# One packed array for constants, norm gains, router weights and biases, and narrower pooling matrices, in a two-layer encoder kernel

## What is computed

```python
for i in range(DEPTH):                                   # DEPTH = 2
    h = rms_norm(x, norm_mix_g[i])
    x = x + (pool_mixer(h, ...) if i == 0 else diff_attention(h, ...))
    h = rms_norm(x, norm_ffn_g[i])
    x = x + hier_moe(h, moe_wg[i], moe_bg[i], moe_we[i], moe_be[i], moe_w1[i], moe_w3[i], moe_w2[i])
return rms_norm(x, final_g)

def pool_mixer(h, w, scale):      # windows 2, 4, 8, 16; 256 channels each
    mix = (cs - lagged) / cnt[None, :, None] - hg        # windowed causal mean minus the token
    outs.append(einsum('bsc,cd->bsd', mix, w[gi]))       # then times scale

def hier_moe(...):
    g_prob = softmax(xf @ wg + bg); e_logits = xf @ we + be   # 4 groups, 8 experts in each
    ...                                                  # top group, top 2 experts in it, gates
    a = silu(xb @ w1[e]) * (xb @ w3[e]); y = a @ w2[e]   # for each expert
```

## Time and profile before

| | |
|---|---|
| runs | 1101.11, 1104.31 and 1104.18 us, median 1104.18 |
| profiled execution, from its first to its last instruction (span) | 1099.3 us |
| median less span | 4.9 us (between 1.8 and 5.0 for the three runs) |
| TensorE busy, mean granted clock | 79%, 0.932 of full speed |
| weight loads of TensorE busy | 47% |
| VectorE, ScalarE, GpSimd busy | 32%, 21%, 0.1% |
| DMA | 426.55 MB, 388 GB/s over the span |

### The profile page before, as it was taken

One profiled execution on the slowest core, in us unless ns is written; L12 is line 12 of the kernel. 1 busy time (PEld: TensorE's weight loads), 2 busy tenths in 40 slices (PEclk: granted clock), 3 DMA queues, 4 the chain that ended last, 5 costly groups with the idle time before them and its releaser, 6 DMA issues.

```text
span 1099.3 us, 18770 instructions
## 1 busy us (share of the span) xinstructions
PE 871.6 (79%) x8132; PEld 512.5 (47%) x8132; DVE 351.2 (32%) x863; ACT 225.6 (21%) x547; POOL 1.2 (0%) x8
## 2 busy tenths in 40 slices
PE   6878776777685868789999988988877766776885
PEld 5744433344343434444787554444534433443442
DVE  3623322323132322222257363322332313232323
ACT  3411211111111111112134332211212111111102
POOL 0000000000000000000000000000000000000000
PEclk9789988989798989999999999999999889897998
DMA  8999999999999999999703678999999999999994
GB/s 343 427 425 424 425 426 427 426 426 427 427 427 427 426 427 427 428 422 421 320 7 120 264 286 361 427 426 426 426 424 425 425 427 427 428 426 427 427 423 191
DMA packets 35587, 426.55 MB, mean 388 GB/s; under 512 B 5394, under 2 KB 6802, under 8 KB 8980
## 3 DMA queue, kind: packets, MB, share of 16 engines
q1 hardware_dynamic: 35476, 424.91, 91.8%
HBM read 423.85 MB, written 1.05 MB: 387 GB/s over the span
## 4 chain that ended last, share of the span: by engine, by line
PE 45%; DMA 38%; DVE 11%; issue 4%; ACT 2%; DVEq 0%; SPq 0%; ACTq 0%
DMA ring<-in_moe_w 37%; PE ps L540 14%; PE ps L588 8%; PE ps L812 5%; PE ps L663 4%; DVE work L1270 3%; PE ps L794 3%; PE ps L473 2%; PE ps L433 2%; PE ps L866 2%; DVE hT L1317 1%; DVE work L1278 1%; PE ps L493 1%; ACT work L986 1%; DVE work L1272 1%
## 5 line engine op out<-in xcount | busy, mean ns | idle before, releaser
L540 PE MATMUL ps<-ring,work 128*32 128x256 f32 x4224 | 284.0, 427 | 137.5 <-DMA ring<-in_moe_w 105.5
L540 PEld LDWEIGHTS ps<-ring,work 128*32 128x32 f32 x4224 | 163.5, 122 | 265.4 <-issue 211.1
L1268 DVE TENSOR_SCALAR work<-work 128x128 f32<-128x128 f32 (+1 forms) x64 | 14.6, 229 | 474.2 <-ACT work L986 474.2
L588 PE MATMUL ps<-ring,work 128*32 128x256 f32 x2032 | 125.2, 388 | 31.6 <-DVE work L1278 30.9
L473 PE MATMUL ps<-work,h_sb 128*128 128x256 f32 x512 | 131.3, 400 | 2.9 <-issue 2.2
L986 ACT ACTIVATE work<-ps 128x256 f32<-128x256 f32 x64 | 24.5, 383 | 504.7 <-PE ps L540 504.7
L1317 DVE COPY hT<-ps 32x512 f32<-32x512 f32 x112 | 76.5, 683 | 133.9 <-PE ps L588 133.1
L473 PEld LDWEIGHTS ps<-work,h_sb 128*128 128x128 f32 x512 | 94.4, 194 | 41.5 <-issue 29.1
L588 PEld LDWEIGHTS ps<-ring,work 128*32 128x32 f32 x2032 | 60.7, 111 | 92.9 <-DVE work L1278 55.5
L998 ACT COPY hT<-ps 32x512 f32<-32x512 f32 x112 | 64.7, 578 | 111.2 <-PE ps L588 110.6
L959 ACT ACTIVATE work<-ps,gcol 128x256 f32<-128x256 f32 (+1 forms) x144 | 58.6, 458 | 110.3 <-PE ps L473 103.9
(11 more groups left out here) (163 smaller groups left out, 467.4 us busy)
## 6 DMA issues: line engine op xcount, KB each, us to landing
ring<-in_moe_w SPq DMA_DIRECT2D x182, 2048.0 KB, 30.5
ring<-in_moe_w SPq DMA_DIRECT2D x15, 1024.0 KB, 30.2
ring<-in_attn_wv SPq DMA_DIRECT2D x2, 2048.0 KB, 33.6
ring<-in_attn_wq SPq DMA_DIRECT2D x2, 2048.0 KB, 32.8
ring<-in_attn_wk SPq DMA_DIRECT2D x2, 2048.0 KB, 33.7
ring<-in_attn_wo SPq DMA_DIRECT2D x2, 2048.0 KB, 36.9
spare<-in_moe_w SPq DMA_DIRECT2D x1, 2048.0 KB, 18.7
x_sb<-in_x SPq DMA_DIRECT2D x2, 512.0 KB, 4.0
```

What stands on the lines that cost most here:

```text
L540: mm = pe.matmul(gu_ps[SB * j:SB * (j + 1), b, :, :], xg[:, u, kt, b, k, :], w[:, :, kt, P * j:P * (j + 1)], start=(kt == 0 and b == 0), s ...
L588: mm = pe.matmul(y_ps[SB * i:SB * (i + 1), b, :], actT[:, b, SB * j:SB * (j + 1)], wj[:, 256 * i:256 * (i + 1)], start=(j == 0 and b == 0) ...
```

## The change

`kernel()` builds two arrays on the host, which only lay inputs and fixed shapes out: `pack` (128 rows of 1568 floats, 784 KB) and `bands` (128 rows of 4 x 272 floats, 544 KB).

* `pack` holds the shape constants, the three norm gains, the router weights of both layers with group and expert columns side by side, and the router biases repeated in each row. One transfer brings it into `cst`; `gcol`, `wr` and `rb` are now parts of `cst`. It takes the place of ten transfers: one for `cst`, three for `gcol`, two for the raw router weights and four bias rows. GpSimd's copies go, and so do the waits at L766, L1047 (now on `cst`), L1194 and the one at L1384.
* The band matrix of a window is zero beyond the 15 columns that spill from half 0 into half 1. Of its cross block 16 columns are kept: a window has 272 columns in place of 384. In the pooling loop the product of 256 columns for half 0 becomes one of 128 and one of 16 columns, so that each of the 8 blocks has three products in place of two.
* SP issues the first half of x ahead of the two rows.

```diff
+            sp.dma_start(x_sb[:, 0, :], x[0, 0:P, :]).then_inc(s_x[0], 16)
             for r, g in enumerate((norm_mix_g[0:1, :], pool_scale[0:1, :])):
                 sp.dma_start(rows[32 * r:32 * r + 1, :], g).then_inc(s_rows, 16)
-            for t in range(TH):
-                sp.dma_start(x_sb[:, t, :], x[0, t * P:(t + 1) * P, :]).then_inc(s_x[t], 16)
-            sp.dma_start(band, consts[:, C_BAND:C_ALL]).then_inc(s_band, 16)
+            sp.dma_start(x_sb[:, 1, :], x[0, P:2 * P, :]).then_inc(s_x[1], 16)
+            sp.dma_start(band, bands).then_inc(s_band, 16)
             sp.dma_start(pw, pool_w[0].rearrange("g (c p) d -> p g c d", p=P)).then_inc(s_pw, 16)
-            sp.dma_start(cst[:, :], consts[:, 0:C_BAND]).then_inc(s_c, 16)
-            for i, g in enumerate((norm_mix_g[1, :], norm_ffn_g[0, :], norm_ffn_g[1, :])):
-                sp.dma_start(gcol[:, i, :], g.rearrange("(p k) -> p k", k=KT)).then_inc(gcol_in, 16)
-            sp.dma_start(wg_raw, moe_wg.rearrange("l (p k) n -> p l (k n)", k=KT)).then_inc(s_wraw, 16)
-            sp.dma_start(we_raw, moe_we.rearrange("l (p k) n -> p l (k n)", k=KT)).then_inc(s_wraw, 16)
-            for layer in range(2):
-                row(rb[:, layer, 0:NG], moe_bg[layer:layer + 1, :]).then_inc(s_rb, 16)
-                row(rb[:, layer, NG:NR], moe_be[layer:layer + 1, :]).then_inc(s_rb, 16)
+            sp.dma_start(cst[:, :], pack).then_inc(s_c, 16)
...
-        @block.gpsimd
-        def _(pool):
-            pool.wait_ge(s_wraw, 32)
...
-                pe.matmul(o, h_sb[:, 0, m * P:(m + 1) * P], band[:, at:at + S], start=True, stop=False)
-                mm = pe.matmul(o[:, P:S], h_sb[:, 1, m * P:(m + 1) * P], band[:, at + S:at + BW], start=False, stop=True)
+                pe.matmul(o[:, 0:P], h_sb[:, 0, m * P:(m + 1) * P], band[:, at:at + P], start=True, stop=True)
+                pe.matmul(o[:, P:S], h_sb[:, 1, m * P:(m + 1) * P], band[:, at + P:at + 2 * P], start=True, stop=False,
+                          skip_group_check=True)
+                mm = pe.matmul(o[:, P:P + SPILL], h_sb[:, 0, m * P:(m + 1) * P], band[:, at + 2 * P:at + BW],
+                               start=False, stop=True, skip_group_check=True)
```

More of the change, by code:

```diff
@@ L63 @@
 C_GROUP = C_PLACE + NE
-C_BAND = C_GROUP + NE
-BW = S + P
-C_ALL = C_BAND + len(WINDOWS) * BW
+C_GCOL = C_GROUP + NE
+C_WR = C_GCOL + 3 * KT
+C_RB = C_WR + 2 * KT * NR
+C_ALL = C_RB + 2 * NR
+SPILL = 16
+BW = 2 * P + SPILL
 FILL_LAST = 1
@@ L75, in shape_constants @@
 def shape_constants():
-    c = np.zeros((P, C_ALL), np.float32)
+    c = np.zeros((P, C_GCOL), np.float32)
+    bands = np.zeros((P, len(WINDOWS) * BW), np.float32)
     i = np.arange(P)
@@ L90, in shape_constants, with by_rows, packed, build @@
         band = ((lag >= 0) & (lag < win)) / np.minimum(t + 1, win)[None, :] - (lag == 0)
[L91 to L98, removed]
+        at = g * BW
+        bands[:, at:at + P] = band[:P, :P]
+        bands[:, at + P:at + 2 * P] = band[P:, P:]
+        bands[:, at + 2 * P:at + BW] = band[:P, P:P + SPILL]
+    return c, bands
+def by_rows(w):
+    return w.reshape(P, KT, *w.shape[1:])
+def packed(inputs):
+    shapes, bands = shape_constants()
+    gains = [inputs["norm_mix_g"][1], inputs["norm_ffn_g"][0], inputs["norm_ffn_g"][1]]
+    parts = [shapes] + [by_rows(np.asarray(g)) for g in gains]
+    for layer in range(2):
+        both = [by_rows(np.asarray(inputs[name][layer])) for name in ("moe_wg", "moe_we")]
+        parts.append(np.concatenate(both, axis=2).reshape(P, KT * NR))
+    for layer in range(2):
+        both = np.concatenate([np.asarray(inputs[name][layer]) for name in ("moe_bg", "moe_be")])
+        parts.append(np.broadcast_to(both, (P, NR)))
+    return {"pack": np.ascontiguousarray(np.concatenate(parts, axis=1)), "bands": bands}
+def build(nc, x, norm_mix_g, pool_w, pool_scale, wq, wk, wv, wo, lq1, lk1, lq2, lk2, subln_g,
+          moe_w1, moe_w3, moe_w2, final_g, pack, bands, out):
     with ExitStack() as ctx:
@@ L116, in build @@
         gain = late[:, 0:D]
-        gcol = sb("gcol", [P, 3, KT])
         rrow = late[:, D:D + 2 * S].rearrange("p (a s) -> p a s", a=2)
-        cst = sb("cst", [P, C_BAND])
+        cst = sb("cst", [P, C_ALL])
+        gcol = cst[:, C_GCOL:C_WR].rearrange("p (i k) -> p i k", i=3)
+        wr = cst[:, C_WR:C_RB].rearrange("p (l k n) -> p l k n", l=2, k=KT)
+        rb = cst[:, C_RB:C_ALL].rearrange("p (l n) -> p l n", l=2)
         work = sb("work", [P, 6144])
         work2 = sb("work2", [P, 2304])
-        wr = sb("wr", [P, 2, KT, NR])
-        rb = sb("rb", [P, 2, NR])
         lam4 = late[:, 1536:1536 + 4 * HD].rearrange("p (a d) -> p a d", a=4)
@@ L145, in build @@
         ones_row = small[:, 832:832 + P]
-        we_raw = work[:, 3584:4096].rearrange("p (l n) -> p l n", l=2)
-        wg_raw = work2[:, 0:64].rearrange("p (l n) -> p l n", l=2)
         band = work[:, 0:len(WINDOWS) * BW]
@@ L199, in build @@
         s_x = [sem("s_x0"), sem("s_x1")]
-        s_c, s_band, s_pw, s_wraw, s_rb, s_lam = (sem(n) for n in ("s_c", "s_band", "s_pw", "s_wraw", "s_rb", "s_lam"))
+        s_c, s_band, s_pw, s_lam = (sem(n) for n in ("s_c", "s_band", "s_pw", "s_lam"))
         s_rows = sem("s_rows")
         s_bc, s_bcc = sem("s_bc"), sem("s_bcc")
-        s_wr = sem("s_wr")
-        gain_in, gcol_in = sem("gain_in"), sem("gcol_in")
+        gain_in = sem("gain_in")
         s_diag, s_rr = sem("s_diag"), sem("s_rr")
@@ L405, in _ @@
             sp.wait_ge(s_out, 64)
-        @block.gpsimd
-        def _(pool):
-            pool.wait_ge(s_wraw, 32)
-            for layer in range(2):
-                pool.tensor_copy(wr[:, layer, :, 0:NG], wg_raw[:, layer, :].rearrange("p (k n) -> p k n", k=KT)).then_inc(s_wr, 1)
-                pool.tensor_copy(wr[:, layer, :, NG:NR], we_raw[:, layer, :].rearrange("p (k n) -> p k n", k=KT)).then_inc(s_wr, 1)
         @block.tensor
@@ L765, in _ @@
             pe.wait_ge(s_c, 16)
-            pe.wait_ge(s_wr, 4)
             for t in range(TH):
@@ L1045, in normalise_tokens @@
                           x_sb[:, t, :].rearrange("p (q k) -> p k q", k=KT), root_x[:, t:t + 1]).then_inc(s_hn, 1)
-            act_e.wait_ge(gcol_in, 48)
+            act_e.wait_ge(s_c, 16)
             norm(1, 0, work[:, 0:D])
@@ L1192, in choose @@
                 ve.wait_ge(s_lg, 2 * layer + t + 1)
-                if layer == 0 and t == 0:
-                    ve.wait_ge(s_rb, 64)
                 then(ve.scalar_tensor_tensor(L, ps[:, LOGITS[t], 0:NR], root_x[:, one], rb[:, layer, :], ALU.mult, ALU.add))
@@ L1383, in _ @@
                 ve.tensor_tensor(x_sb[:, t, :], x_sb[:, t, :], h_sb[:, t, :], ALU.add).then_inc(s_x2, 1)
-            ve.wait_ge(gcol_in, 48)
             ve.wait_ge(s_c, 16)
@@ L1493, in _ @@
                                             ALU.mult, ALU.mult).then_inc(s_h, 1)
-_INS = ["x", "norm_mix_g", "norm_ffn_g", "pool_w", "pool_scale", "attn_wq", "attn_wk", "attn_wv", "attn_wo",
-        "attn_lq1", "attn_lk1", "attn_lq2", "attn_lk2", "attn_subln_g", "moe_wg", "moe_bg", "moe_we", "moe_be",
-        "moe_w1", "moe_w3", "moe_w2", "final_g"]
+_INS = ["x", "norm_mix_g", "pool_w", "pool_scale", "attn_wq", "attn_wk", "attn_wv", "attn_wo",
+        "attn_lq1", "attn_lk1", "attn_lq2", "attn_lk2", "attn_subln_g", "moe_w1", "moe_w3", "moe_w2", "final_g"]
 def kernel(**inputs):
@@ L1506 @@
     arrays, args = {}, []
-    for name in _INS + ["consts"]:
-        a = shape_constants() if name == "consts" else np.ascontiguousarray(inputs[name])
+    laid_out = packed(inputs)
+    for name in _INS + ["pack", "bands"]:
+        a = laid_out[name] if name in laid_out else np.ascontiguousarray(inputs[name])
         arrays[f"in_{name}"] = a
```

## The result

The changed kernel takes 1109.32 us (median of 6 runs, 1104.17 to 1111.26), beside 1103.95 us of the kernel before: ratio 1.0047, 95% interval 1.0026 to 1.0068. It is slower, by 5.4 us. The forecast was 1101.2, with 1104.6 as the upper end. Its profiled execution has a time of 1110.21 and a span of 1108.4 us, 9.1 above the span before.

What follows compares the result with a forecast made beforehand. The DMA stream was taken to bound both layers, with attention at TensorE's pace between. Gains of 0.6 + 0.5 + 1.9 = 3.0 us at chunk 0 took 1104.18 to 1101.2 us, range 1097.8 to 1104.6.

Steps and rivals of the forecast that it cites:

- term 3: DMA stream at the head: one packed transfer for ten brings chunk 0 in 1.9 us earlier, bounds 1.3 to 2.0.
- the 0.5 us of the narrower bands: DMA stream at the head: 0.229 MB less to load saves 0.54 us at 425 GB/s.
- either way it is off the path: Pooling loop: three products cost 0.65 us a block as before, and their price does not touch the path to chunk 0.
- up to 1.9 us may come back: First pooling products: half pace follows 4.0 us without work; that gap shrinks to about 2, returning up to 1.9 us.
- rival C: Hole in the DMA queue at chunk 8 if the first slot frees over 1.5 us later: 1102.7 us, chance 0.08.
- the rows behind half 0: Broadcasts at the head: the first ends at 6.2, the second at 8.1; pooling starts 0.4 us earlier to 0.3 later.
- The slack: Chunk 8, issued at the first freed slot: lands 12.2 us later, could land in 7.7, so 4.5 us to spare.
- lead: DMA stream: chunk 0 lands 3.0 us earlier, and this is carried through to the last landing of layer 0.
- Term 1: Head of the DMA stream: issuing half 0 of x first gains 0.6 us at chunk 0, between 0.3 and 0.69.
- B': Moved TensorE code adds one more pause where layer 1's loads are issued at TensorE's pace: 1103.8 us, chance 0.10.

Runs made afterwards that it cites:

- the zeros: The changed kernel, rows first, plus four 512-column products of zeros between broadcasts and pooling: 1100.93 us with three products a block, 1102.11 us with two narrow ones.
- the delay: The kernel before with 12 products of zeros (512 columns each) on TensorE just ahead of the transposes, nothing else changed: 1108.2 us, ratio 1.0048.

## Why the prediction was wrong

**Right.** What bounds the kernel: each us at chunk 8 is a us at the end of layer 0. Also that a packed transfer gives back the gap behind the small ones (term 3 said 1.9, at most 2.0; pack only moved chunk 0 by 2.4 and the last of layer 0 by 2.3; that the rows of the bands were taken for 3 KB, where 768 KB over 128 rows are 6 KB, changes nothing in the sum), the 0.5 us of the narrower bands (chunk 0 at 17.3 for 17.8, with rows first), and SP's issue of chunk 0 (4.3 for the 4.5 forecast). With two narrow products and the rows first the stream gained 2.7 to 2.9 us and the kernel 1.7 to 4.0 (ratios 0.9985 with the zeros, 0.9979 and 0.9964 without): about the forecast of 3.0, but in another kernel than the one forecast.

**The step that failed: "either way it is off the path".** I priced the three products at full pace, 0.65 us a block, and that price holds (0.66 with the zeros ahead). But the row beside it showed that pooling starts at half pace. I took it that the pace would come back as before, or sooner because the gap before it shrinks, and booked "up to 1.9 us may come back". In both executions of the changed kernel and in two experiments with three products and no zeros it did not come back in ten us. At half pace three products cost 1.28 us a block throughout, 3.2 us more in pooling, and 2.0 to 2.2 more in the products behind in three of the four. The chance of this, rival C's "low pace throughout", I put at 0.08.

**The second half of that step: the rows behind half 0.** I let VectorE go on when the first broadcast ends, at half of the 3.79 us. The earlier trace rows say otherwise: VectorE's step starts at 6.58, which is the end of both. The records come in pairs that start together and take over 1 us each, the two broadcasts side by side:

```profile
L439 PE MATMUL ps<-work,small x2: 1189/1202/1216, 2.8 to 2.8; 1*128 1x512 f32 x2
```

This is the kernel before; the row was there to be read. So the whole 1.6 us of the rows went into the head, and pooling began 1.4 us later, not "0.4 us earlier to 0.3 later".

**The slack was mis-sized, and its far side left out.** I had 12.2 - 7.7 = 4.5 us. One execution came near 7.7 (7.8, with the delay), but in the seven others in which the slot decided when chunk 8 lands it took 9.4 to 9.9, so the slack was about 2.5. A lead of 1.6 to 3.0 uses that up almost by itself. And I let rival C lose only the lead ("the lead shrinks to what the slack allows, 1 to 2 us"). With slot 0 at 54.8 chunk 8 can't land before 64.2 to 64.7, whatever the lead: the loss has no floor at zero. Done with my own numbers, 6.3 us of delay against 4.5 of slack gives a loss of 1.8; with the slack of 2.5, 3.8; measured 4.0.

**Term 1, half 0 of x first, has the wrong sign.** Chunk 0 came later with it, in four pairs that differ by the order: 18.6 for 17.3, 18.6 for 17.8, 18.7 for 17.6 and 21.6 for 20.2. In the changed kernel the bytes of 4 to 8 us are 1.16 MB at 291 GB/s, for 1.59 MB at 397 before; the other pairs are alike (297 for 403, 279 for 365, 346 for 397 GB/s). Why the early transfers flow slower in that order no run tells. By chunk 7 the difference is 0 to 1.5.

**B', more pauses at the start of layer 1.** All four profiles of kernels with three products and no zeros show a pause of 1.9 to 2.0 us at 662 to 666, 161 to 162 us behind the start of attention's first products, ahead of one of 2.1 to 2.6 at 672 to 676. The chain of three other kernels at the same stage: zeros with two narrow products, zeros with three products, and delay only.

```profile
661.99 0.35 issue
669.14 2.44 issue
...
661.71 1.28 issue
...
668.12 1.29 issue
```

Sorted by how many products TensorE's code has more than before, the pauses over 0.3 us between 155 and 180 us behind attention's start are: none more (seven profiles), one of 2.5 to 2.6 at 169 to 171; four more, 0.35 and 2.44; eight more (four profiles), 1.9 to 2.0 and 2.1 to 2.6; twelve more, one of 1.28 or 1.29 at 161 to 163. The two with twelve more share little but that number: one is the kernel before with the delay, one has the packed array and three products. So code length does move pauses, and with eight more products they add up to 4.0 to 4.6 us here, for 2.5 to 2.6. Whether it costs the time is open: from the last landing of layer 0 to that of layer 1 it was 593.8, 594.6, 596.3 and 598.2 us in these four and 592.8 to 597.1 in the others, and attention's first products took 10.54 us in most profiles, 12.23 or 12.93 in five, with no relation to the edit. The part of the changed kernel's 5.4 us beyond the 4.0 of layer 0 (or of its 3.7 beyond 1.8, when it was run again) can't be put to one cause.

## What to carry to other kernels

Where a stream is fed through a ring, find the first load that waits for a slot and compare two times: when the load ahead of it lands, and when it could land itself if issued when its slot comes free. Only the first of the two moves with a faster head of the stream; the second is a matter of the compute head, and past the point where they meet every us there is lost for good. Price short products at both paces, by what the engine did just before, and where an edit cuts columns keep the number of products: two of 144 and 128 columns gave the same narrow bands without the loss, and with the packed array and the rows ahead of x the fastest kernel here.

## What the runs showed of the hardware

- Eight blocks of three short products (128, 128 and 16 columns) started at half pace and stayed there for 10.2 to 10.3 us in four profiles; the same columns as two products of 144 and 128 came up after 3.9 to 5.8 us in three; started at full pace, the three stayed at full pace for 5.3 us. The PEclk column of the changed kernel stands at 1.00 in these 10 us, though each product takes twice its later time, so durations had to be read, not that column. Later in the head the column does show it: it reads 0.50 while the products of the first gathers take 3.76 us, where those of the second take 2.02:

```profile
40.00:45.00 5.00, 3.55 (x16) 3.31 (x17) 4.24 (x23) 2.26 (x2) 0.00 (x0) 0.50 0.99 423
```

- The Trainium skill ("TensorE: Matmul & The Clock Gate", Part 1) says that the clock stands at half rate by default and that activity releases it. The durations of the kernels with two products a block agree (1.3 us a block at first, 0.65 later, in the kernel before); the three products did not bring the full pace back while they ran.
- A 2 MB load into an emptying queue, with one more issued 0.4 us behind it, landed 9.4 to 9.9 us after its issue in seven executions, whether the load ahead of it landed 1.2 us before that issue or 4.1 us after it, and 7.8 us after it in one (1.5 us before). What makes the difference no run tells.
- Two sets of products with one row each (K = 1), from partitions 0 and 32, ran side by side: their records start in pairs, 4 pairs in the kernel before, and both sets end with the last pair at 6.5 to 6.6 us, so the first result was there no earlier than the second.
